# Memory attention of a hybrid encoder block by head over 512 tokens, with split value products

## The reference, cut to what matters

```python
def _memory_attention(qx, mem_k, mem_v):
    b, s = qx.shape[:2]
    scores = jnp.einsum('bshd,bmhd->bhsm', qx, mem_k).astype(jnp.float32) * (X_HEAD_DIM ** -0.5)
    probs = jax.nn.softmax(scores, axis=-1).astype(mem_v.dtype)
    return jnp.einsum('bhsm,bmhd->bshd', probs, mem_v).reshape(b, s, X_WIDTH)
```

## Time and profile before

| | us |
|---|---|
| median of 3 runs | 2591.36 |
| lowest to highest | 2590.91 to 2592.15 |
| the profiled execution's own time | 2593.32 |
| its span | 2591.5 |

### The profile page before, as it was taken

How to read it: one execution, slowest core, us unless ns; L and a number is a source line. 1 busy time by engine, 2 the same in 40 slices (tenths; PEclk the granted TensorE clock), 3 DMA queues, 4 the chain that set the end, 5 groups by cost and what they waited for, 6 DMA issues and landing times.

```text
span 2591.5 us, 33051 instructions
## 1 busy us (share of the span) xinstructions
PE 2565.0 (99%) x12065; PEld 2128.1 (82%) x12065; DVE 1734.6 (67%) x2401; ACT 1157.6 (45%) x2131; POOL 551.3 (21%) x510
## 2 busy tenths in 40 slices
PE   8999999999999999999999999999999999999998
PEld 7888888888887887888887888888888888888887
DVE  7778657666466655658778666765557566575886
ACT  6344535344344433434456455654555243342533
POOL 1455200000022152336554333000000112111100
PEclk9999999999999999999999999999999999999999
DMA  4778555666446787787797666633355585767753
GB/s 146 253 241 258 199 183 179 186 216 225 144 136 240 236 258 256 230 276 260 231 298 230 229 220 197 218 110 118 110 172 162 114 221 109 185 150 161 201 179 114
DMA packets 346764, 508.71 MB, mean 196 GB/s; under 512 B 33208, under 2 KB 213484, under 8 KB 346604
## 3 DMA queue, kind: packets, MB, share of 16 engines
q1 hardware_dynamic: 318956, 431.08, 51.5%
q0 software_dynamic: 27648, 75.51, 11.8%
HBM read 325.12 MB, written 181.40 MB: 195 GB/s over the span
## 4 chain that ended last, share of the span: by engine, by line
PE 93%; DVE 4%; issue 1%; ACT 1%; DMA 1%; POOL 0%; SPq 0%; POOLq 0%; DVEq 0%
PE ps L2416 29%; PE ps L2418 29%; PE ps L2417 29%; PE ps L2421 2%; PE ps L2693 1%; PE ps L2670 1%; PE ps L2438 1%; DVE res_lo L1653 1%; DVE s_lo L1647 1%; PE ps L2593 1%; PE ps L2621 1%; DMA res_raw<-in_w_down 0%; DMA proj_d<-c 0%; ACT scores L1123 0%; DVE res_lo L1641 0%
## 5 line engine op out<-in xcount | busy, mean ns | idle before, releaser
L2416 PE MATMUL ps<-res_hi,s_hi 128*128 128x512 f32 x3084 | 1204.3, 391 | 6.4 <-issue 1.7
L2418 PE MATMUL ps<-res_hi,s_lo 128*128 128x512 f32 x3084 | 1200.9, 389 | 0.0
L2417 PE MATMUL ps<-res_lo,s_hi 128*128 128x512 f32 x3084 | 1200.9, 389 | 0.0
L2416 PEld LDWEIGHTS ps<-res_hi,s_hi 128*128 128x128 f32 x3084 | 579.1, 188 | 130.0 <-issue 6.1
L2418 PEld LDWEIGHTS ps<-res_hi,s_lo 128*128 128x128 f32 x3084 | 579.0, 188 | 120.7
L2417 PEld LDWEIGHTS ps<-res_lo,s_hi 128*128 128x128 f32 x3084 | 579.2, 188 | 118.1
L1123 ACT ACTIVATE s_hi<-piece_f 128x512 fp32r<-128x512 f32 x436 | 274.3, 631 | 478.6 <-PE ps L2418 420.6
L1123 ACT ACTIVATE s_hi<-s_sum 128x512 fp32r<-128x512 f32 x327 | 204.1, 628 | 367.5 <-PE ps L2418 338.6
L1647 DVE TENSOR_TENSOR s_lo<-piece_f,s_hi 128x512 fp32r<-128x512 f32 x432 | 322.6, 747 | 34.5 <-ACT s_hi L1123 26.5
L1647 DVE TENSOR_TENSOR s_lo<-s_sum,s_hi 128x512 fp32r<-128x512 f32 x327 | 247.8, 758 | 87.9 <-ACT s_hi L1123 87.7
L1707 DVE TENSOR_TENSOR u<-u,ps 128x512 f32<-128x512 f32 x109 | 74.8, 686 | 294.5 <-PE ps L2418 294.4
(11 more groups left out here) (195 smaller groups left out, 2501.7 us busy)
## 6 DMA issues: line engine op xcount, KB each, us to landing
proj_d<-c SPq DMA_DIRECT2D x152, 256.0 KB, 3.3
piece_f<-in_w_up SPq DMA_DIRECT2D x32, 1024.0 KB, 6.8
up_d<-c SPq DMA_DIRECT2D x128, 256.0 KB, 3.3
piece_f<-up_d SPq DMA_DIRECT2D x32, 1024.0 KB, 7.0
piece_f<-in_w_gate SPq DMA_DIRECT2D x24, 1024.0 KB, 7.1
w_hi<-parts_d SPq DMA_DIRECT2D x48, 512.0 KB, 3.7
w_lo<-parts_d SPq DMA_DIRECT2D x48, 512.0 KB, 5.2
temp<-proj_d SPq DMA_DIRECT2D x48, 512.0 KB, 6.8
```

The costliest lines, as they stand in the source:

```text
L2416: mm(dst, wh, xh, start=first, stop=False, skip_group_check=joins)
L2417: mm(dst, wh, xl, start=False, stop=False, skip_group_check=joins)
L2418: return mm(dst, wl, xh, start=False, stop=last, skip_group_check=joins)
```

## The change

Now a memory step takes one head and all 512 tokens of the block. Scores are still four matmuls of 256 columns, one for each group of 128 tokens. The eight transposes put the first 128 memory tokens of all 512 tokens in bank 6 and the second 128 in bank 7. The value products become two `product` calls, six float32r matmuls of 512 columns. For this the transposed probabilities are split: ACT writes the high part `m_pt_hi` (two instructions of 512 columns, as the copies before), and DVE writes the low part `m_pt_lo` in a new function `mpt_low` (two subtractions of 512 columns), for which the value products wait (`mpl_rdy`). The memory values are split once, `mem_values_high` on ACT and `mem_values_low` on DVE, in block 0. `mem_scale` is two instructions of 512 columns instead of one of 1024, and `mem_across` waits for each half. In the last memory branch product of the first quarter (`branch_part`), the split of the work is by head (three heads, then one) with 512 columns, and no longer by token groups (384 columns, then 128). Some semaphores are merged (`setup`, `pad_rdy`, `misc_done`, `late_ld`).

```diff
-    m_pt = there("m_pt", [P, NXH, MT, P], 108)
+    m_pt_hi = there("m_pt_hi", [P, MT, TB], 108, F32R)
+    m_pt_lo = there("m_pt_lo", [P, MT, TB], 68, F32R)
+    mem_v_lo = there("mem_v_lo", [P, MT, 4 * P], 136, F32R)
+    mem_v_hi = [there(f"mem_v_hi{t}", [P, 4 * P], kb, F32R) for t, kb in enumerate((170, 184))]
...
+            def mem_values_high():
+                act.wait_ge(qm_ld, 64)
+                for s in range(4):
+                    act.wait_ge(up_st[s], 16 * IN_END)
+                for t in range(MT):
+                    last = op(mem_v_hi[t][:], mem_v[:, t, :], ACT.Copy)
+                last.then_inc(mvh_rdy, 1)
...
                 act.wait_ge(mt_done, k + 1)
-                for z in range(2):
-                    last = op(m_pt[:, 2 * z:2 * z + 2].rearrange("p h m n -> p (h m n)"), ps[:, ATT + 2 + z, :], ACT.Copy)
-                last.then_inc(mpt_rdy, 1)
+                for t in range(MT):
+                    op(m_pt_hi[:, t, :], ps[:, ATT + 2 + t, :], ACT.Copy).then_inc(mpt_rdy, 1)
...
                         y0_high(3)
+                        mem_values_high()
...
+            def mpt_low(k):
+                for t in range(MT):
+                    dve.wait_ge(mpt_rdy, MT * k + t + 1)
+                    last = v.tensor_tensor(m_pt_lo[:, t, :], ps[:, ATT + 2 + t, :], m_pt_hi[:, t, :].bitcast(F32), ALU.subtract)
+                last.then_inc(mpl_rdy, 1)
...
-                chained(v.reciprocal(rd[:, 0:NXH], den[:, 0:NXH]))
-                v.tensor_tensor(m_scores[:], m_scores[:], per_row(rd, NXH, NMEM), ALU.mult).then_inc(mp_rdy, 1)
+                chained(v.reciprocal(rd[:, 0:TT], den[:, 0:TT]))
+                for f in range(2):
+                    half = m_scores[:, 2 * f:2 * f + 2, :]
+                    v.tensor_tensor(half, half, rd[:, 2 * f:2 * f + 2].rearrange("p (h o) -> p h o", o=1)
+                                    .broadcast_to([P, 2, NMEM]), ALU.mult).then_inc(mp_rdy, 1)
...
             def local(b):
                 k = TT * b
+                mpt_low(k - 1)
                 att_max(k)
                 y2_low(k - 1)
...
                 if j:
+                    mpt_low(4 * b + j - 1)
                     mem_max(b, j)
...
+                mpt_low(4 * NBLK - 1)
                 y2_low(4 * NBLK - 1)
...
-                c = slice(steps[0] * P, steps[1] * P)
-                for k in range(4):
+                c = slice(steps[0] * P, steps[1] * P) if r == 0 else slice(0, TB)
+                for k in range(4) if r == 0 else range(*steps):
...
-                for h in range(NXH):
-                    last = mm(ps[:, ATT + h // 2, (h % 2) * NMEM:(h % 2 + 1) * NMEM],
-                              q_mem[:, h, j * P:(j + 1) * P], mem_k[:, h, :], start=True, stop=True)
+                for t in range(TT):
+                    last = mm(ps[:, ATT + t // 2, (t % 2) * NMEM:(t % 2 + 1) * NMEM],
+                              q_mem[:, j, t * P:(t + 1) * P], mem_k[:, j, :], start=True, stop=True)
...
             def mem_values(b, j):
-                pe.wait_ge(mpt_rdy, 4 * b + j + 1)
-                for h in range(NXH):
-                    for t in range(MT):
-                        last = mm(ps[:, ATT + 2, h * P:(h + 1) * P], mem_v[:, t, h * P:(h + 1) * P], m_pt[:, h, t, :],
-                                  start=t == 0, stop=t == MT - 1)
+                pe.wait_ge(mpl_rdy, 4 * b + j + 1)
+                if b == j == 0:
+                    pe.wait_ge(mvl_rdy, 1)
+                c = slice(j * P, (j + 1) * P)
+                for t in range(MT):
+                    last = product(ps[:, ATT + 2, :], mem_v_hi[t][:, c], mem_v_lo[:, t, c], m_pt_hi[:, t, :], m_pt_lo[:, t, :],
+                                   t == 0, t == MT - 1)
                 last.then_inc(mv_done, 1)
```

More of the change, by code:

```diff
@@ L337, in build @@
     v_tm = there("v_tm", [P, NCH, P], 72)
-    m_scores = there("m_scores", [P, NXH, NMEM], 76)
+    m_scores = there("m_scores", [P, TT, NMEM], 76)
     w_hi = there("w_hi", [P, WS, 4, PC], 80, F32R)
     temp = there("temp", [P, GS, 2, TB], 92)
-    m_pt = there("m_pt", [P, NXH, MT, P], 108)
+    m_pt_hi = there("m_pt_hi", [P, MT, TB], 108, F32R)
+    m_pt_lo = there("m_pt_lo", [P, MT, TB], 68, F32R)
     k_pad = there("k_pad", [P, CHUNK + TB], 112)
@@ L432, in build @@
     mpt_rdy = sem("mpt_rdy")
+    mpl_rdy = sem("mpl_rdy")
+    mvh_rdy = sem("mvh_rdy")
+    mvl_rdy = sem("mvl_rdy")
     mv_done = sem("mv_done")
@@ L2554, in pool_rows_across @@
                     last = transpose(ps[:, 6, g * P:(g + 1) * P], wp_st[:, g, :])
-                last.then_inc(wp_tr, 1)
+                last.then_inc(misc_done, 1)
             def fuse_pool(u):
@@ L2681, in mem_across @@
                     pe.wait_ge(y0_done, 4 * (b + 1))
-                for h in range(NXH):
-                    for t in range(MT):
-                        c = (h % 2) * MT + t
-                        last = transpose(ps[:, ATT + 2 + h // 2, c * P:(c + 1) * P], m_scores[:, h, t * P:(t + 1) * P])
+                for f in range(2):
+                    pe.wait_ge(mp_rdy, 2 * k + f + 1)
+                    for i in range(2 * f, 2 * f + 2):
+                        for t in range(MT):
+                            last = transpose(ps[:, ATT + 2 + t, i * P:(i + 1) * P], m_scores[:, i, t * P:(t + 1) * P])
                 last.then_inc(mt_done, 1)
             def mem_values(b, j):
-                pe.wait_ge(mpt_rdy, 4 * b + j + 1)
-                for h in range(NXH):
-                    for t in range(MT):
-                        last = mm(ps[:, ATT + 2, h * P:(h + 1) * P], mem_v[:, t, h * P:(h + 1) * P], m_pt[:, h, t, :],
-                                  start=t == 0, stop=t == MT - 1)
+                pe.wait_ge(mpl_rdy, 4 * b + j + 1)
+                if b == j == 0:
+                    pe.wait_ge(mvl_rdy, 1)
+                c = slice(j * P, (j + 1) * P)
+                for t in range(MT):
+                    last = product(ps[:, ATT + 2, :], mem_v_hi[t][:, c], mem_v_lo[:, t, c], m_pt_hi[:, t, :], m_pt_lo[:, t, :],
+                                   t == 0, t == MT - 1)
                 last.then_inc(mv_done, 1)
```

44 lines of the change are left out of this document (21 added, 23 removed).

## The result

| | before | changed |
|---|---|---|
| median, us | 2591.07 (6 runs) | 2605.97 (6 runs) |
| lowest to highest, us | 2589.86 to 2592.15 | 2604.19 to 2608.58 |
| ratio of the times, 95% interval | | 1.0058 (1.0045 to 1.0071) |
| span of the profiled execution, us | 2591.5 | 2605.0 |

A forecast was written before the change was run, and what follows sets the result against it. The prediction took TensorE to bound the kernel in the mixers. Its terms, −3.6 + 3.6 + 7.6 − 0.3 − 0.5 = +6.8 us, took the median from 2591.4 to 2598.2 us, with a range of 2594.0 to 2603.5.

The forecast's parts named there:

- What bounds it: In the mixers TensorE is busy 334.5 of 336 us, so time saved or waited there counts in full.
- the value products: Each memory step: six matmuls at 0.23 us, 1.38 us instead of 1.79; gain 0.41 us a step.
- The ordinary step: Steps 1 and 2 of blocks 0 to 2, steps 1 to 3 of block 3: 0.40 us gained each, −3.6 us.
- a start 0.17 later costs nothing: Ordinary step: `mem_scale` is held until GpSimd's addition ends anyway, so its start 0.17 us later loses nothing.
- The step behind `pool_mean`: Step 3 of blocks 0 to 2: TensorE waits for late low parts and `y2_low`; 1.21 us lost each, +3.6 us.
- A: The start of a memory step's `mem_across` (the transposes), from which times in that step are counted in us.
- The start of a block: Blocks 1 to 3: TensorE stands still about 3.5 us for `mpt_low`; 2.54 us lost each, +7.6 us.
- So nothing more is lost in `local`: Block start: `att_max` and `y2_low`, though late, are done before TensorE needs them, so no further loss.
- Rival 3: TensorE's pace falls behind its new pauses of about 3.5 us: 1.6 us each, three times, 2603.0 us; chance 0.10.
- First transposes of block 3 and the end: Shorter wait for `mem_scale` at block 3, −0.3 us; VectorE's chain to the output job starts earlier, −0.5 us.
- Rival 1: Low parts are ready when TensorE wants them at block starts, all waits stay hidden: 2583.3 us; chance 0.06.
- rival 2: Only block starts cost; the step behind `pool_mean` goes like an ordinary one: +2.0 us, 2593.4 us; chance 0.12.

The follow-up runs named there:

- experiment 7: Experiment 5 with GpSimd's window sums for blocks 2 and 3 cut to 16 columns each: 2587.02 us; the same cut in the kernel before: 2590.89 us.
- experiment 5: Experiment 1 with the four `pool_mean` instructions spread over two places each of steps 2 and 3: 2588.89 us, ratio 0.9990.
- experiment 2: The changed kernel with 14 extra matmuls, result unread, in TensorE's pause at the start of blocks 1 to 3: 2598.68 us, ratio 1.0027.
- experiment 8: Experiment 5 with `mean_part` and ScalarE's `pool_parts` earlier and two of four `pool_low` subtractions ahead of `mpt_low`: 2586.51 us; with `mem_scale` also one instruction: 2587.50 us.
- experiment 1: The changed kernel with `mpt_low` moved ahead of `pool_low` at the end of a block: 2593.33 us, ratio 1.0007.
- experiment 3: The kernel before, with two unused VectorE subtractions behind `pool_low` for which the value products wait at blocks 1 to 3: 2604.69 us, ratio 1.0049.

## Why the prediction was wrong

**What bounds it, and the value products: right.** Every new wait of TensorE came out in full, and the six matmuls have the pitch of 0.23 us.

**The ordinary step: right in block 0, wrong in two blocks.** Block 0's steps gained 0.44 and 0.41, those of block 3 0.37 to 0.42. But step 1 of blocks 1 and 2 lost 0.42 and 0.40, and step 2 gained only 0.20 and 0.23. The step that failed is "a start 0.17 later costs nothing": I read one step, in block 0, and took it nine times. In blocks 1 and 2 GpSimd's sums hold VectorE, the copies, `mpt_low` and `mem_max` start later, and the slack of some 0.1 us that block 0 has (`y2_low` ends at 858.70, `mem_across` starts at 858.77) is not enough. 2.0 us of the miss; experiment 7 gives them back. The Trainium skill, "SBUF — State Buffer", section "Who interferes with whom", says that an instruction of VectorE with two inputs in SBUF contends with one of GpSimd that reads SBUF, that certain copies and scalings can contend with GpSimd too, and that one with at most one input in SBUF otherwise does not. The trace agrees: the scaling of `m_scores` went from 1.29 to 2.15 and 2.68 us and `nb` from 0.17 to 0.53, while `mpt_low`, which has one input in PSUM and one in SBUF, and `mem_max`, which reads PSUM alone, kept 1.29 and 1.21.

**The step behind `pool_mean`: right.** The value products start at A + 5.63 (forecast 5.64), the next `mem_across` at A + 11.07 (forecast 11.10), and experiment 5 removes the wait by its named cause.

**The start of a block: the wait right, its price wrong, and this decides.** The wait ended at A + 6.51 (forecast 6.5) and TensorE stood still for 3.46 us (forecast about 3.5). The step that failed is "So nothing more is lost in `local`". It followed which instruction would be late next, and not how fast TensorE would be behind the pause. Rival 3 is what happened: by the medians the lower clock costs 2605.97 − 2598.68 = 7.3 us; in the traces the block starts of the change exceed those of experiment 2 by 2.86, 1.60 and 1.34, 5.8 us together. The three stretches at half clock, 6.8 + 3.4 + 3.4 = 13.6 us, cost at most half of that, 6.8, and at most 6.3 once the 0.6 and 0.5 us that fall into the pauses themselves are left out. So the trace's 5.8 is the better figure, and the 7.3 agrees with it within the noise. Rival 3 had priced it at 4.8 and had a chance of 0.10. What I set against it, that 3.5 us is half of the 7.1 at the kernel's start, was no evidence: TensorE's waits in the trace of before have none between 7.1 us and the next longest, so nothing in it said that 3.5 us is harmless:

```profile
PE ps L2438 <- POOL diag L2219: 1.7, 1, 1.7
```

And its price rested on a pace from the kernel's start over an assumed 4 us; the real stretch behind the first pause was longer and its pace lower (0.43 against 0.23 us for a matmul). With no row for either, the range had to reach further up than 2603.5. The Trainium skill, "TensorE: Matmul & The Clock Gate", section "Why this matters for your kernels", warned of just this: pauses between bursts of matmuls bring the clock back to half. Here the trace agrees: 0.50 behind the pauses of 3.5 us, 1.00 behind that of 1.65.

**First transposes of block 3 and the end: right.** In experiment 2 block 3's start is 0.36 cheaper than the two others (forecast 0.3), and from the last `mem_across` to the product of the output job that waits for VectorE the change gains 0.48 (forecast 0.5). TensorE itself gets to the first product of that job 1.53 us earlier (forecast 1.5), and the difference is lost in that wait, as forecast.

Rival 1 (all hidden) and rival 2 (only the block start costs) are out: the waits for `m_pt_lo` and for `y_lo` stand in the first list above.

In the traces the sum is 7.2 us over the forecast: 5.8 by the clock and 2.0 by the held steps, less 0.6 for losses at the starts and behind `pool_mean` that were smaller than forecast. The medians lie 7.8 over it, and their interval is 3.4 us wide to either side, so the times cannot fix the parts more closely. In the prediction's own sum, +3.9 and +9.9 give 2595.3 to 2601.3 and not quite the 2594 to 2602 that it names; nothing hangs on that.

The gain of the value products is real: steps without a new wait are 0.37 to 0.44 us shorter. With `mpt_low` and `pool_mean` in other places (experiment 5) the kernel is 2.5 us faster than the one before, by an interval that just excludes no change. The 4.7 us of experiment 8 are not all due to the change, since its edit also moves pooling work for which the kernel before waited; that edit was not tried in the kernel before.

## What to carry to other kernels

Where a change makes TensorE stand still for some microseconds, look up the granted clock behind every pause of that length in the trace, and if there is none, price the pause as its length plus half of a stretch at half clock: here a pause of 3.5 us made a block's start 2.5 us longer by itself, and another 1.3 to 2.9 by the lower clock behind it. Put a new instruction of an in-order engine ahead of the work that has slack: one moved call (experiment 1) was worth 12.6 us, the fall of the clock included. And read a repeated step in each of its surroundings before multiplying it: what another engine does beside it can use up its slack.

## What the hardware showed that I had not expected

The granted clock fell to 0.50 behind a pause of only 3.5 us, and stayed there for 6.8 us once and 3.4 us twice in the changed kernel, and for 3.4 us three times in experiment 3, at the same places and with nearly the same work ahead. I did not settle what makes the first one longer. A pause of 1.65 us behind seven matmuls did not lower it. At the kernel's start the pace was 12 matmuls in two us where 20 came later, with a granted clock of 1.00 in the windows; so there the record did not show what the pace did, and that stays open too.
